# A two-layer decoder trunk on eight cores: fewer weight copies behind the gating stage, LayerNorm statistics and affines moved between engines

## The reference, cut to what matters

```
for i in (0, 1):                                   # two layers
    h = x * (1 + scale) + shift                    # from the conditioning c
    y = sliding_window_attention(h) if i == 0 else chunked_spatial_gating(h)
    x = layer_norm(ALPHA * x + (1 + gate) * y, g, b)
    h = x * (1 + scale2) + shift2
    y = hierarchical_moe(h)                        # 4 groups x 8 experts, top 2 of one group
    x = layer_norm(ALPHA * x + (1 + gate2) * y, g, b)

def chunked_spatial_gating(h):
    z = gelu(h @ w_in + b_in)                      # 1024 -> 4096
    u, v = split(z)                                # 2048 each
    v = layer_norm(v, sgu_g, sgu_b)                # per token, over 2048
    mixed = tril(w_s) @ v + b_s                    # inside chunks of 128 tokens
    return (u * mixed) @ w_out + b_out

def layer_norm(x, g, b):
    mu = mean(x); var = mean(square(x - mu))
    return (x - mu) * rsqrt(var + 1e-5) * g + b
```

## Time and profile before

| | |
|---|---|
| time, median of 3 runs | 2141.79 us (2138.82 to 2142.64) |
| the profiled execution | 2141.08 us |
| span of its slowest core (core 1), which the profile shows | 2139.8 us |
| spans of all cores | 2083.6 to 2139.8 us |
| busy: TensorE / VectorE / ScalarE / POOL | 1309.1 / 1141.0 / 712.8 / 665.9 us |
| DMA of the core | 337.71 MB, mean 158 GB/s |

### The profile page before, as it was taken

One profiled execution on the slowest core, in us unless ns is written; L12 is line 12 of the kernel. 1 busy time (PEld: TensorE's weight loads), 2 busy tenths in 40 slices (PEclk: granted clock), 3 DMA queues, 4 the chain that ended last, 5 costly groups with the idle time before them and its releaser, 6 DMA issues.

```text
span 2139.8 us, 32161 instructions; the slowest of 8 cores (2083.6 to 2139.8 us)
## 1 busy us (share of the span) xinstructions
PE 1309.1 (61%) x9811; PEld 807.0 (38%) x9811; DVE 1141.0 (53%) x2761; ACT 712.8 (33%) x1340; POOL 665.9 (31%) x630
## 2 busy tenths in 40 slices
...
GB/s 164 178 141 145 170 153 140 145 143 127 141 196 208 172 176 176 162 156 159 148 120 127 131 134 111 142 120 131 114 154 111 196 41 216 188 241 225 236 164 211
DMA packets 96982, 337.71 MB, mean 158 GB/s; under 512 B 28353, under 2 KB 29189, under 8 KB 87064
## 3 DMA queue, kind: packets, MB, share of 16 engines
...
## 4 chain that ended last, share of the span: by engine, by line
DMA 42%; PE 26%; DVE 11%; issue 11%; ACT 6%; POOL 2%; another core or an unknown queue 1%; DVEq 0%; ACTq 0%; POOLq 0%; SPq 0%
DMA wbf<-moe_w 17%; PE bank L1288 7%; DMA rbuf<-m_ys,m_ids 6%; DMA m_XS<-hrow,m_ids 4%; PE bank L1040 3%; DMA sb_W<-gmlp_w_in 3%; PE bank L1306 3%; PE bank L1129 2%; ACT n_hTe L1271 2%; DMA sb_W<-ada_w 2%; DMA sb_W<-moe_w 2%; PE bank L1264 2%; PE bank L767 2%; POOL rbuf L1314 1%
## 5 line engine op out<-in xcount | busy, mean ns | idle before, releaser
L528 POOL DMA_DIRECT2D wbf<-moe_w x132 | 69.8, 530 | 503.1 <-DMA wbf<-moe_w 200.6
L1288 PE MATMUL bank<-m_hTe,sb_W 128*128 128x256 bf16 x1024 | 152.6, 316 | 48.2 <-DMA sb_W<-moe_w 33.2
L1677 PE MATMUL bank<-g_hTg,sb_W 128*128 128x256 bf16 x1024 | 129.7, 286 | 62.4 <-ACT g_uT L1682 62.1
L1646 PE MATMUL bank<-sb_W,g_hTg 128*128 128x512 bf16 x512 | 139.2, 420 | 37.1 <-ACT g_hTg L1630 31.2
L1271 ACT ACTIVATE m_hTe<-bank,sb_H_ 128x256 bf16<-128x256 f32 x192 | 94.3, 563 | 165.6 <-PE bank L1264 152.8
L1288 PEld LDWEIGHTS bank<-m_hTe,sb_W 128*128 128x128 bf16 x1024 | 113.8, 113 | 82.9 <-issue 54.8
L1288 PE MATMUL bank<-n_hTe,sb_W 128*128 128x256 bf16 x1024 | 133.6, 289 | 18.7 <-ACT n_hTe L1271 18.3
L1309 DVE SCALAR_TENSOR_TENSOR m_ys<-bank,m_wv,m_gt 128x512 f32<-128x512 f32 x128 | 88.5, 745 | 105.9 <-DMA rbuf<-m_ys,m_ids 79.6
L1677 PEld LDWEIGHTS bank<-g_hTg,sb_W 128*128 128x128 bf16 x1024 | 102.9, 103 | 82.8 <-issue 65.4
L1314 POOL DMA_INDIRECT rbuf<-m_ys,m_ids x64 | 100.8, 1575 | 101.3 <-DMA rbuf<-m_ys,m_ids 57.5
L1271 ACT ACTIVATE n_hTe<-bank,sb_H_ 128x256 bf16<-128x256 f32 x192 | 94.2, 562 | 110.2 <-PE bank L1264 101.2
...
## 6 DMA issues: line engine op xcount, KB each, us to landing
wbf<-moe_w POOLq DMA_DIRECT2D x132, 512.0 KB, 41.6
...
sb_W<-ada_w POOLq DMA_DIRECT2D x36, 512.0 KB, 13.5
sb_W<-xin SPq DMA_DIRECT2D x16, 512.0 KB, 14.3
rbuf<-sb_W SPq DMA_DIRECT2D x16, 512.0 KB, 13.6
...
g_zt<-rbuf SPq DMA_DIRECT2D x16, 512.0 KB, 13.6
```

The source lines that it names most:

```text
L528: e.dma_start(out=out, in_=in_), reads=reads, writes=writes, adds=adds, proc=proc, after=after)
L1288: S.op("pe", lambda e, f=f, k=k, fb=fb: e.matmul(banks[bk][:, f * 256:(f + 1) * 256], wgu[:, k, fb:fb + 128], hTe[i3][:, k, :], start=(k = ...
L1646: S.op("pe", lambda e, k=k, c=c, bk=bk: e.matmul(banks[bk][:], hTg[:, k, i2 * 128:(i2 + 1) * 128], wvv[:, c, k, :], start=(k == 0), stop=F ...
L1677: S.op("pe", lambda e, f=f, fb=fb, k=k: e.matmul(banks[bk][:, f * 256:(f + 1) * 256], wuv[:, fb // 4, k, (fb % 4) * 128:(fb % 4 + 1) * 128 ...
```

## The change

It does five things.

1. The set of copied positions of layer 1 becomes 2 to 25: 24 experts, 72 copies. Positions 0, 1 and 26 to 31 are loaded by `wload` on POOL's queue, as most of layer 0's are.
2. The copies get a DMA process of their own, `dp`. In gating each of the places calls `spot()`, which issues a copy at 72 of every 126 calls, evenly spread; what is left is issued at the end.
3. `affine3` is gone; `C`, `finish_tile` in gating and the last stage use `affine`.
4. In `V` the sum of v comes out of the `Gelu` (`accum_out`), and the sum of squares about the mean out of two `Square` passes on ScalarE over 1024 elements each. They write their unused output into `vh`. `bn_stats` and `bn_aggr` of v are gone.
5. In the last stage three tiles in four get their statistics from ScalarE (`stats_act`: a `Copy` and a `Square` pass, each with a sum, then Ln and Exp); the fourth keeps `bn_stats`.

```
-        for p in (..., "dg", "dl"):
+        for p in (..., "dg", "dl", "dp"):
-        pre = [set(range(2, 14)), set(range(NE))]
+        pre = [set(range(2, 14)), set(range(2, 26))]
...
-                    dma("pool", "dw", wbf[l, ex]...
+                    dma("pool", "dp", wbf[l, ex]...
...
+        def stats_act(z, bz, junk, bjunk, w, bw):
+            S.op("act", lambda e: e.activation(out=junk, in_=z, func=AF.Copy, accum_out=w[:, 0:1]), ...)
+            ts(w[:, 1:2], w[:, 0:1], -1.0 / D, None, ALU.mult, None, [bw], [bw])
+            S.op("act", lambda e: e.activation(out=junk, in_=z, func=AF.Square, bias=w[:, 1:2], accum_out=w[:, 2:3]), ...)
+            S.op("act", lambda e: e.activation(out=w[:, 0:1], in_=w[:, 2:3], func=AF.Ln, scale=1.0 / D, bias=eps_t[:]), ...)
+            S.op("act", lambda e: e.activation(out=w[:, 3:4], in_=w[:, 0:1], func=AF.Exp, scale=-0.5), ...)
...
-            affine3(z, bz, mv[:, 0:1], bmv, rs, brs, A1, BA1, A0, BA0)
+            affine(z, bz, mv[:, 0:1], bmv, rs, brs, A1, BA1, A0, BA0)
...
+        def spot():
+            n_spot[0] += 1
+            if n_spot[0] * 72 // 126 > (n_spot[0] - 1) * 72 // 126:
+                next(casts[1], None)
...
-                        next(casts[1], None)
+                        spot()
                     S.op("act", lambda e, c=c, q=q, bk=bk: e.activation(
-                        out=v32[q][...], in_=banks[bk][:], func=AF.Gelu),
-                         reads=[PB[bk]], adds=[Bv32[q]])
-                    S.op("dve", lambda e, c=c, q=q: e.bn_stats(out=gst[i2][:, c, :], in_=v32[q][...]), ...)
+                        out=v32[q][...], in_=banks[bk][:], func=AF.Gelu,
+                        accum_out=gst[i2][:, c:c + 1]), reads=[PB[bk]], adds=[Bv32[q], Bgst[i2]])
-            S.op("dve", lambda e: e.bn_aggr(out=mv[:], in_=gst[i2]), ...)
-            rs, brs, nm, bnm = rstd_newton(0, mv, bmv)
+            red(g8[:, 4:5], g8[:, 0:4], ALU.add, [bg8], [bg8])
+            ts(g8[:, 5:6], g8[:, 4:5], -1.0 / 2048, None, ALU.mult, None, [bg8], [bg8])
+            for h in range(2):
+                S.op("act", lambda e, h=h, q=vq[h]: e.activation(
+                    out=vh[i2][:, h * 1024:(h + 1) * 1024], in_=v32[q], func=AF.Square, bias=g8[:, 5:6],
+                    accum_out=g8[:, 6 + h:7 + h]), reads=[Bv32[vq[h]], bg8], writes=[bg8], adds=[Bvh[i2]])
+            ts(mv[:, 0:1], g8[:, 5:6], -1.0, None, ALU.mult, None, [bg8], [bmv])
+            tt(mv[:, 1:2], g8[:, 6:7], g8[:, 7:8], ALU.add, [bg8], [bmv])
+            S.seal(Bvh[i2])
+            rs, brs, nm, bnm = rstd_newton(0, mv, bmv, 1.0 / 2048)
...
+        for _ in casts[1]:
+            pass
...
         def o_a(t):
+            if t % 4 != 3:
+                w, bw = ow[t % 4], Bow[t % 4]
+                stats_act(zo[t % 8], Bzo[t % 8], jk[t % 2], Bjk[t % 2], w, bw)
+                st[t] = w, bw
+                return
...
         def o_b(t):
+            if t % 4 != 3:
+                w, bw = st[t]
+                stt(z, z, w[:, 1:2], A1, ALU.add, ALU.mult, [bz, bw, BA1], [bz])
+                stt(z, z, w[:, 3:4], A0, ALU.mult, ALU.add, [bz, bw, BA0], [bz])
+            else:
+                rs, brs, nm, bnm = st[t]
+                affine(z, bz, mv_[t % 4][:, 0:1], Bmv_[t % 4], rs, brs, A1, BA1, A0, BA0)
```

More of the change, by code:

```diff
@@ L440, in build @@
         S = Sched(nc, es)
[L441 removed]
+        for p in ("dx", "dw", "dc", "do", "ds", "dh", "dm", "dr", "dy", "dg", "dl", "dp"):
             S.dma_proc(p)
@@ L657, in affine @@
             stt(z, z, rs, A0, ALU.mult, ALU.add, [bz, brs, BA0], [bz])
-        def affine3(z, bz, mu, bmu, rs, brs, A1, BA1, A0, BA0):
-            stt(z, z, mu, A1, ALU.subtract, ALU.mult, [bz, bmu, BA1], [bz])
-            S.op("act", lambda e: e.activation(out=z, in_=z, func=AF.Copy, scale=rs), reads=[bz, brs], writes=[bz])
-            tt(z, z, A0, ALU.add, [bz, BA0], [bz], eng="pool")
+        def stats_act(z, bz, junk, bjunk, w, bw):
+            S.op("act", lambda e: e.activation(out=junk, in_=z, func=AF.Copy, accum_out=w[:, 0:1]), reads=[bz], writes=[bjunk, bw])
+            ts(w[:, 1:2], w[:, 0:1], -1.0 / D, None, ALU.mult, None, [bw], [bw])
+            S.op("act", lambda e: e.activation(out=junk, in_=z, func=AF.Square, bias=w[:, 1:2], accum_out=w[:, 2:3]),
+                 reads=[bz, bw], writes=[bjunk, bw])
+            S.op("act", lambda e: e.activation(out=w[:, 0:1], in_=w[:, 2:3], func=AF.Ln, scale=1.0 / D, bias=eps_t[:]),
+                 reads=[bw, Beps], writes=[bw])
+            S.op("act", lambda e: e.activation(out=w[:, 3:4], in_=w[:, 0:1], func=AF.Exp, scale=-0.5), reads=[bw], writes=[bw])
         def route_bufs(P):
```

29 lines of the change are left out of this document (15 added, 14 removed).

## The result

| | before | change |
|---|---|---|
| median of 7 runs | 2142.64 us (2138.82 to 2178.66) | 2116.39 us (2105.14 to 2129.52) |
| change / before, 95% interval | | 0.9883 [0.9841, 0.9925] |
| the profiled execution | 2141.08 us | 2105.14 us |
| span of its slowest core | 2139.8 us (core 1) | 2103.8 us (core 2) |

The change is faster by 1.2%, 26 us; 90 were forecast, and 2116 lies outside the range of 2010 to 2095. The profiled execution is the fastest of the seven.

A forecast was written before the change was run, and what follows sets the result against it. Expert copies, HBM to HBM, were taken to pace POOL, and POOL the tiles in gating. Six steps -92.6, second MoE layer +6 and last stage -3.5 took 2141.1 to 2051 us; range 2010 to 2095.

The forecast's parts named there:

- the stall of rows 5: Gating: a load behind a POOL add came late; VectorE stood 20.6 us, TensorE idled 24.3; forecast to go.
- Copies at 4.83 us, 54 us of DMA a step: Gating steps: 9.7 copies at 4.83 us plus 7 make 54 us of DMA, so POOL keeps up.
- Step period 66: Gating, m = 1 to 6: each step takes 66 us, 396 against 488.6 in all, -92.6 us.
- "Cost 0" for the statistics of v: Gating, `V`: statistics about 2 us longer in sequence, hidden by 10 us before TensorE uses v; cost 0.
- ScalarE is tied to VectorE: Rival, `Square` passes in `V`: passes wait for VectorE's sum, 24.3 us stalls in six steps; 2197 us, 4%.
- VectorE in a step: Gating: `bn_stats` and `bn_aggr` out, second affine products and small operations in; net -0.2 us, counted as nothing.
- shorter steps: Rival, gating: POOL adds stretch VectorE products on TensorE's path; without them period 60, another 6 x 6; 2015 us, 12%.
- The second MoE layer +6: Six more direct expert loads cost +6 us, between 0 and 23, with gathers of 30 experts before the first.
- the rival that had 10%: Second MoE layer turns DMA-bound, direct loads at their upper bound, +17 on the forecast; 2068 us, 10%.
- Last stage -3.5: Last stage: POOL's adds go, first product starts later, 53.5 us of VectorE work left; -3.5 us, between -8 and +3.
- Square and tables: Gating: `Square` at 1.15 us, readouts 0 to 0.2 us each; rival of two table loads per tile, 2082 us, 2%.
- m = 0 at 0: Gating, first step: stays as it is, since it waits for the gating weights; 0 us.

The follow-up runs named there:

- e6: The kernel before with only the copies' spacing changed: all 96, evenly spread, in their own process `dp`; 0.9789 of the kernel before, m = 1 to 6 442.7 us.
- e4: The change with all 96 copies, evenly spread, and no direct load in the second MoE layer; 0.9713 of the kernel before, m = 1 to 6 442.5 us.
- e3: The change with `bn_stats` and `bn_aggr` of v back on VectorE; 0.9679 of the kernel before, m = 1 to 6 419.8 us.
- e7: The change with its six direct loads at positions 9, 13, 17, 21, 25, 29 instead of 26 to 31; 0.9786 of the kernel before, MoE 311.3 us.
- e8: e3 with the `Gelu` operations still writing their sums to a tile nobody reads; 0.9728 of the kernel before, m = 1 to 6 421.2 us.
- e1: The kernel before with only 72 evenly spread copies and six more direct loads, arithmetic unchanged; 0.9822 of the kernel before, m = 1 to 6 437.7 us.

## Why the prediction was wrong

The forecast was 65 us too low. By its steps, on the slowest cores of the profiles: the six steps +44, the second MoE layer +16, m = 0 +3, the last stage -5, the time up to gating -5, the median above the profiled execution +11. (Up to gating the lists of the two kernels are the same; the means of the fourteen profiles lie between 991 and 1003 us there.) The text's own sign of being wrong, periods above 75, came in the even steps: 76.4 to 76.8.

- **The mechanism was right.** The copies left the chain of waits, POOL's waits for them went from 200.6 us to none, the stall of rows 5 did not return, with z tiles on time. e6 shows that this is worth 43 us.
- **Copies at 4.83 us, 54 us of DMA a step: right that it would not bind, wrong about why.** It counted the fewer copies as the cure. 13 a step, 69 us by the same sum, are as good (e4). That 17 (89 us) did not fit and 13 do in steps of 70 to 77 us is what the sum would have said, had it been made for other counts too.
- **Step period 66: the failed step, in two terms.** It took TensorE's own work plus the end of each step from the first step of before, and let one number stand for all. An odd step without the passes is 66.4 us as a mean (e3), as forecast; an even one 73.5. The routing batch was read off as 70.5 against 67.2, in a step where neither a POOL add nor a second product of the affine stands in its chain. The sum put the new second products at nothing, by VectorE's busy time; ahead of the logits and in the routing chain TensorE waits for them. Three even steps x 7.5 = 22 us.
- **"Cost 0" for the statistics of v: the second term, 22 us.** v comes 4 us later as a mean (6 in the steps shown), not 2, for a pass waits for VectorE and VectorE for the pass. The cover of 10 us was real, but it was looked for at TensorE alone; the cost goes by what stands behind the waits on VectorE's list. The text asked that for ScalarE's list (the `Gelu` of the next tile) and not for VectorE's. It is the rival "ScalarE is tied to VectorE" with 3.6 us a step where 24.3 had been set, without a late tile. Part of the 3.6 is the granted clock behind a longer wait, which the sum did not have.
- **VectorE in a step: net 0 in busy time, and 18 to 25 us gained.** The rival "shorter steps" named the stretch under POOL's adds; on the path it lies on operations of 0.2 us, in the routing chain (1 us) and ahead of `g_mt`, and the scaling that left ScalarE's list has a part too. The Trainium skill (GPSIMD Engine Reference, Specifications) states that POOL shares SBUF interfaces with VectorE and contends with VectorE instructions that have two SBUF inputs. For such an instruction the trace agrees, with 2.34 for 0.19 us. Of that rival's 36 us half to two thirds are there, hidden by what the passes cost.
- **The second MoE layer +6: too low by 16.** "Near the lower end for that order" was a choice, and the order was what made it dear: the gathers stand before the six loads, but scatter-adds stand between and behind. The upper bound, 23 us, was nearly reached: +22.1 on the slowest core (+15.9 as a mean). This is the rival that had 10%. The Trainium skill (DMA: Bandwidth & Descriptors, Queues, rings and completion order) states, where it speaks of the queues of SP and ACT, that descriptors are consumed in ring order on each DMA engine. On POOL's queue e7 fits the same: with as many loads, set apart, 17 us go, and no more is left than the 312.8 of before.
- **Last stage -3.5: -8.3.** The first product came 26.0 us after the last product with the gates (2049.60 less 2023.65), 6.5 later than before, where 4.8 was forecast. The work behind it took 46.9 us, not 53.5: the products and `bn_stats` are 46 as counted, the small operations and gaps about 1 and not 7.
- **Square and tables:** the passes take 1145 ns, as costed, with no table load in the steps. A readout is an instruction of 0.19 us, the upper bound taken; where nobody waits for the sums it costs next to nothing (e8, 1.4 us in six steps).
- **m = 0 at 0: +3 to +8.** It is 97 with the old arithmetic (e1, e6), 102 to 103 with the affine, 104 to 107 with the passes (103 with raw squares). Which wait makes it stays open.
